# Two layers of a hybrid decoder trunk: scans moved out of the first inverse, and memory pieces dealt anew

## The reference

```python
for l in range(2):
  p = rmsnorm(x, norm_mix[l]) @ w_in[l]           # 1024 -> 3592 columns, split over four mixers
  y_a = hgrn2_mixer(...)      # group A: gated linear recurrence, 4 heads x 64
  y_b = gated_deltanet(...)   # group B: (I + lower) u = rhs per chunk of 64 tokens: a triangular inverse
  y_c = rglru_mixer(...)      # group C: h_t = a_t h_{t-1} + u_t, a = exp(-8 r softplus(-lambda))
  y_d = rwkv7_mixer(...)      # group D: decay w = exp(-exp(-0.5) sigmoid(.)), a second inverse
  x = x + concat(y_a, y_b, y_c, y_d) @ w_out[l]
  mem_n = rmsnorm(mem); k = mem_n @ wk[l]; v = mem_n @ wv[l]
  x = x + softmax(q k^T / 16) v @ wo[l]           # q = rmsnorm(x) @ wq[l], 4 heads x 256
  x = x + (swiglu(rmsnorm(x)) if l == 0 else top2_of_8_experts(rmsnorm(x)))
out = rmsnorm(x, norm_final)
```

## Time and profile before

| | us |
|---|---|
| median of 3 runs | 1963.12 (1962.64 to 1963.27) |
| profiled execution, own time | 1961.31 |
| its span, first to last instruction | 1959.5 |
| PE busy | 1861.4 (95%) |
| DVE busy | 1465.5 (75%) |
| ACT busy | 1121.3 (57%) |

### The profile page before, as it was taken

The page is one execution under the profiler, slowest core; times in us unless marked ns, Lnnn a source line. Parts: engine busy times, 40 slices in busy tenths (PEclk is TensorE's granted clock), DMA queues, the critical chain, the costliest instruction groups (busy, mean ns, idle before and its releaser), DMA issues.

```text
span 1959.5 us, 29713 instructions
## 1 busy us (share of the span) xinstructions
PE 1861.4 (95%) x12520; PEld 1605.6 (82%) x12521; DVE 1465.5 (75%) x1543; ACT 1121.3 (57%) x1057; POOL 0.2 (0%) x4
## 2 busy tenths in 40 slices
PE   7997899999999978999699999999999999999996
PEld 6986789899989866897588888888888888888884
DVE  6778645554467687453789989889899898998985
ACT  5563134434344641244567777677776777767774
POOL 0000000000000000000000000000000000000000
PEclk9998999999999989999899999999999999999998
DMA  7520234355555212243599999989999999999992
GB/s 243 172 75 15 66 108 165 108 181 185 194 157 164 89 45 66 74 164 111 184 393 342 373 330 384 370 335 371 337 383 365 335 372 348 369 364 339 369 373 97
DMA packets 239450, 465.99 MB, mean 238 GB/s; under 512 B 11856, under 2 KB 87760, under 8 KB 239312
## 3 DMA queue, kind: packets, MB, share of 16 engines
q1 hardware_dynamic: 239312, 464.03, 66.4%
HBM read 462.95 MB, written 1.05 MB: 237 GB/s over the span
## 4 chain that ended last, share of the span: by engine, by line
PE 88%; DVE 9%; issue 1%; ACT 1%; DMA 1%; DVEq 0%; SPq 0%; ACTq 0%
PE ps L2148 31%; PE ps L1617 16%; PE ps L2158 16%; PE ps L1602 12%; PE ps L1637 8%; DVE MT L907 2%; PE ps L2204 2%; PE ps L2179 1%; PE ps L1682 1%; PE ps L2219 1%; DVE MT L913 1%; DVE TMP L907 1%; DVE MT L910 1%; DMA raw<-in_w_in 1%; DVE spare_hi L907 0%
## 5 line engine op out<-in xcount | busy, mean ns | idle before, releaser
L1380 DVE TENSOR_TENSOR wlo<-raw,whi 128x2048 fp32r<-128x2048 f32 x140 | 320.5, 2292 | 55.7 <-ACT whi L787 55.4
L787 ACT ACTIVATE whi<-raw 128x2048 fp32r<-128x2048 f32 x140 | 268.9, 1922 | 121.1 <-PE ps L2158 71.3
L920 DVE TENSOR_TENSOR wlo<-raw,whi 128x2048 fp32r<-128x2048 f32 x85 | 194.6, 2289 | 85.3 <-ACT whi L480 85.1
L1380 DVE TENSOR_TENSOR wlo<-PT,whi 128x2048 fp32r<-128x2048 f32 x84 | 192.1, 2293 | 31.2 <-ACT whi L787 30.1
L480 ACT ACTIVATE whi<-raw 128x2048 fp32r<-128x2048 f32 x85 | 162.1, 1907 | 64.7 <-PE ps L1637 36.6
L2148 PE MATMUL ps<-whi,hE_hi 128*128 128x512 f32 x672 | 185.5, 398 | 2.4 <-DVE hE_lo L1449 2.4
L787 ACT ACTIVATE whi<-PT 128x2048 fp32r<-128x2048 f32 x84 | 161.5, 1922 | 34.9 <-PE ps L2148 34.2
L2148 PE MATMUL ps<-wlo,hE_hi 128*128 128x512 f32 x672 | 180.2, 390 | 0.0
L2148 PE MATMUL ps<-whi,hE_lo 128*128 128x512 f32 x672 | 179.9, 390 | 0.0
L2148 PEld LDWEIGHTS ps<-wlo,hE_hi 128*128 128x128 f32 x672 | 126.2, 188 | 27.1
L2148 PEld LDWEIGHTS ps<-whi,hE_lo 128*128 128x128 f32 x672 | 126.2, 188 | 26.5
(11 more groups left out here) (297 smaller groups left out, 3356.7 us busy)
## 6 DMA issues: line engine op xcount, KB each, us to landing
raw<-in_moe_w_up SPq DMA_DIRECT2D x111, 1024.0 KB, 7.0
PT<-in_moe_w_down SPq DMA_DIRECT2D x56, 1024.0 KB, 6.5
PT<-in_moe_w_gate SPq DMA_DIRECT2D x55, 1024.0 KB, 6.9
TMP<-in_moe_w_gate SPq DMA_DIRECT2D x55, 1024.0 KB, 6.8
raw<-in_moe_w_down SPq DMA_DIRECT2D x55, 1024.0 KB, 6.1
raw<-in_w_in SPq DMA_DIRECT2D x28, 1024.0 KB, 5.3
raw<-in_ffn_w_gate SPq DMA_DIRECT2D x11, 1024.0 KB, 5.3
raw<-in_ffn_w_up SPq DMA_DIRECT2D x11, 1024.0 KB, 5.7
```

The costliest lines, as they stand in the source:

```text
L787: nc.scalar.activation(ex_hi[m % XSPL], ex_raw[m % XRAW], ACT.Copy).then_inc(S("w_hi"), 1)
L920: V.tensor_tensor(wlo[i % SPL][:, :], raw[d % RAW][:, :], whi[i % SPL][:, :].bitcast(F32), ALU.subtract).then_inc(S("w_lo"), 1)
L1380: V.tensor_tensor(ex_lo[m % XSPL], ex_raw[m % XRAW], ex_hi[m % XSPL].bitcast(F32), ALU.subtract).then_inc(S("w_lo"), 1)
```

## The change

- **Group C's polynomial** (`rglru`) is renumbered: the slices that ran at v = 0 to 3 of the `hgrn` loop now run at j = 9, 10 and 11 behind the `w_in` chunks (as v = -4, -3, -2); one product moves from v = 4 to v = 6. The scan itself, with its output, moves from v = 4 of the first inverse to behind the second inverse, ahead of the split of `w_out` chunk 1, with a `chain.settle()` after it. Its buffers move from `whi` to `wlo` of the same slot.
- **Group D's decay scans** (one scaling, four scans, one small negation) move from v = 1 of the first inverse to j = 12, ahead of `logs`. The scaling K_KK moves from DVE to ACT.
- **Group A's outputs** go to PSUM bank 6 instead of 7, and ACT copies them to SBUF (`h_out`), so bank 7 is free for memory pieces.
- **Memory pieces.** Layer 1's piece order is v0, k0 to k3, v1 to v3. Its piece 0 is computed in the norm of layer 0's feed-forward part, its piece 1 in the first norm of layer 1: half before and half after the turning products. Piece 2 lies in the `hgrn` loop (half before it, one k step in v = 1 to 4), 3 and 4 in the first inverse, 5 in group B's solves, none in the second inverse, 6 and 7 as before. In layer 0 pieces 0 and 1 lie in the `hgrn` loop, 2 and 3 in the first inverse, 4 to 7 as before.
- **Start.** The table of small parameters is loaded by a transfer issued from ACT rather than SP, and the small activations of group C's lambda and group B's A_log, with two more table loads, run on ACT before the first statistics instead of in layer 0's `logs`; the six small DVE instructions behind them move to `rglru(l, -4)`.

The diff, cut to its core:

```diff
+PIECES = [[("xattn_wk", j) for j in range(4)] + [("xattn_wv", j) for j in range(4)],
+          [("xattn_wv", 0)] + [("xattn_wk", j) for j in range(4)] + [("xattn_wv", j) for j in range(1, 4)]]
 def plan_chunks():
...
+        if layer:
+            out += kv[1][1:2]
         out += [("cm", "w_in", layer, c) for c in W_IN_COLS]
-        out += pieces[0:4] + w_out[0:1] + pieces[4:6] + w_out[1:2] + pieces[6:7] + w_out[2:4] + pieces[7:8]
+        out += kv[layer][2 * layer:4 + layer] + w_out[0:1] + kv[layer][4 + layer:6] + w_out[1:2] + kv[layer][6:7] + w_out[2:4] + kv[layer][7:8]
...
         if layer == 0:
+            out += kv[1][0:1]
...
-        KV_BANK = [[7, 6, 7, 7, 7, 7, 2, 1], [7, 6, 7, 7, 7, 7, 2, 3]]
+        KV_BANK = [[7, 6, 7, 7, 7, 7, 2, 1], [3, 1, 7, 7, 7, 7, 2, 3]]
@@ ACT
-                a(tmp(5), ps[:, 7, :], ACT.Square).then_inc(S("o_sq"), 1)
-                act.wait_ge(S("rk_kk"), l + 1)
+                a(tmp(5), ps[:, 6, :], ACT.Square)
+                a(h_out(l), ps[:, 6, :], ACT.Copy).then_inc(S("o_sq"), 1)
+                for c in range(2):
+                    s_ = slice(256 * c, 256 * c + 256)
+                    a(K_KK[:, s_], pt(D_K)[:, s_], ACT.Copy, scale=pc("rwkv_k_k", l, c))
                 a(K_RN, K_KK, ACT.Square).then_inc(S("rk_sq"), 1)
...
             def deltanet(l):
+                kv_put(l, 2 + l)
                 rwkv_ahead(l)
...
+            act.dma_start(par[:, :], A["params"]).then_inc(S("par_in"), 16)
+            table("exp_and_others")
+            act.wait_ge(S("par_in"), 16)
+            for k in range(DEPTH):
+                o, o2 = PCOL["gdn_A_log", k][0], PCOL["lru_lambda", k][0]
+                a(col(lam[k], 2), par[:, o2:o2 + 2], ACT.Abs)
+                a(col(expa[k], 4), par[:, o:o + 4], ACT.Exp)
+                a(col(lam[k], 2), col(lam[k], 2), ACT.Exp, scale=-1.0)
+            table("natural_log")
+            for k in range(DEPTH):
+                a(col(lam[k], 2), col(lam[k], 2), ACT.Ln, bias=1.0).then_inc(S("lam_sp"), 1)
             table("sqrt_and_others")
@@ DVE, gates_ahead
+                    rglru(l, -4)
                 if j == 10:
+                    rglru(l, -3)
...
+                if j == 11:
+                    rglru(l, -2)
...
+                    dve.wait_ge(S("lora_s"), l + 1)
+                    ts(pt(C_X), pt(C_X), -float(np.exp(-0.5)), ALU.mult)
+                    for i in range(4):
+                        s_ = slice(P * i, P * i + P)
+                        chain.link(lambda: V.tensor_tensor_scan(K_B[:, s_], ones, pt(C_X)[:, s_], 0.0, ALU.mult, ALU.add))
+                    ts(col(ST_NC0, 4).unsqueeze(2), many(K_B)[:, :, HD - 1:HD], -1.0, ALU.mult)
                     logs(l)
@@ DVE, deltanet and rwkv
-                    if v == 4:
-                        rglru(l, LEVELS)
...
                 inverse(2 * l + 1)
+                rglru(l, LEVELS)
+                chain.settle()
                 ahead(first_chunk["w_out", l] + 2)
@@ PE, hgrn
-                kv(l, 0, range(KT // 2))
+                kv(l, 2 * l, range(KT // 2))
...
-                    if v < 5:
-                        kv(l, (v + 1) // 2, range(KT // 2) if v % 2 else range(KT // 2, KT))
+                    if l and 1 <= v < 5:
+                        kv(1, 2, [v + 3])
+                    if l == 0 and v < 2:
+                        kv(0, 0, range(5, 8) if v else [4])
+                    if l == 0 and 2 <= v < 6:
+                        kv(0, 1, [2 * v - 4, 2 * v - 3])
...
+                kv(l, 2 + l, [0])
@@ PE, first inverse
                     if v == 0:
+                        kv(l, 2 + l, [1])
                         head_ss(l, 0, tmp(5))
+                        kv(l, 2 + l, [2, 3])
                     if v == 1:
...
+                        kv(l, 2 + l, [4, 5])
+                    if v == 2:
+                        kv(l, 2 + l, [6, 7])
                     if v >= 3:
-                        pe.wait_ge(S("y_put"), 4 * l + 1)
-                        kv(l, 3, range(2 * v - 6, 2 * v - 4))
+                        pe.wait_ge(S("kv_put"), 2 * NH * l + 3 + l)
+                        kv(l, 3 + l, range(2 * v - 6, 2 * v - 4))
@@ PE, second inverse
-                    kv(l, 5, [v, v + 1] if v == LEVELS - 1 else [v])
+                    if l == 0:
+                        kv(0, 5, [v, v + 1] if v == LEVELS - 1 else [v])
@@ PE, norms
             def swiglu():
+                kv(1, 0, range(PRE))
                 pe.wait_ge(S("x_done"), 4)
                 norm(3)
+                kv(1, 0, range(PRE, KT))
...
+                if l:
+                    kv(1, 1, range(PRE))
                 norm(norm_index(l))
+                if l:
+                    kv(1, 1, range(PRE, KT))
```

More of the change, by code:

```diff
@@ L266, in lru, with h_out @@
         def lru(l, k):
-            return spare[0][(first_chunk["w_in", l] + 12) % SPL][:, 512 * k:512 * k + 512]
+            return spare[1][(first_chunk["w_in", l] + 12) % SPL][:, 512 * k:512 * k + 512]
+        def h_out(l):
+            return spare[0][(first_chunk["w_in", l] + 12) % SPL][:, 0:512]
         def h_state(l):
@@ L533, in gates_ahead @@
                     mem_norm(j)
+                if l and j == 1:
+                    kv_put(1, 1)
                 if j == 6:
@@ L592, in logs @@
                 a(col(ST_SP, 8), col(ST_SP, 8), ACT.Exp, scale=-1.0)
-                if l == 0:
-                    for k in range(DEPTH):
-                        o, o2 = PCOL["gdn_A_log", k][0], PCOL["lru_lambda", k][0]
-                        a(col(lam[k], 2), par[:, o2:o2 + 2], ACT.Abs)
-                        a(col(expa[k], 4), par[:, o:o + 4], ACT.Exp)
-                        a(col(lam[k], 2), col(lam[k], 2), ACT.Exp, scale=-1.0)
                 table("natural_log")
@@ L601, in logs @@
                     a(tmp(5), tmp(5), ACT.Ln, bias=1.0).then_inc(S("hg_ln"), 1)
-                    for k in range(DEPTH):
-                        a(col(lam[k], 2), col(lam[k], 2), ACT.Ln, bias=1.0)
                 else:
@@ L636, in hgrn @@
                         a(tmp(2), ps[:, 4, :], ACT.Exp).then_inc(S("gd_eg"), 1)
-                        kv_put(l, 0)
                     if v == 2:
@@ L647, in hgrn @@
                         rel_part(l, 0)
-                        kv_put(l, 1)
+                        if l == 0:
+                            kv_put(0, 0)
                     if v == 4:
@@ L654, in hgrn @@
                         a(h_kdt(l), ps[:, 5, 0:256], ACT.Copy).then_inc(S("hg_kd"), 1)
-                        kv_put(l, 2)
+                    if v == 6:
+                        kv_put(l, 1 + l)
                 table("natural_log")
@@ L700, in deltanet @@
                 ahead(first_chunk["w_out", l] + 1)
-                kv_put(l, 3)
+                kv_put(l, 3 + l)
                 for t in range(TT):
@@ L705, in deltanet @@
                 head_rms(l)
-                kv_put(l, 4)
+                kv_put(l, 4 + l)
                 ahead(first_chunk["w_out", l] + 2)
@@ L711, in rwkv @@
                 a(tmp(5), ps[:, 6, :], ACT.Copy).then_inc(S("rk_vk"), 1)
-                kv_put(l, 5)
+                if l == 0:
+                    kv_put(0, 5)
                 for t in range(TT):
@@ L762, in swiglu @@
                     ahead(n + SPL)
+                    if j == 0:
+                        kv_put(1, 0)
                     act.wait_ge(S("chunk_done"), n + 1)
@@ L1188, in hgrn, with head_out @@
                 take(LEVELS - 1)
-            def head_out(l, which, bank, o, gain, gate, pair):
+            def head_out(l, which, src, o, gain, gate, pair):
                 dve.wait_ge(S("o_rn"), 2 * l + which + 1)
-                tt(o, ps[:, bank, :], o, ALU.mult)
+                tt(o, src, o, ALU.mult)
                 for c in range(2):
@@ L1238, in rwkv_ahead @@
                         s_ = slice(256 * c, 256 * c + 256)
-                        ts(K_KK[:, s_], pt(D_K)[:, s_], pc("rwkv_k_k", l, c), ALU.mult).then_inc(S("rk_kk"), 1 if c else 0)
-                    for c in range(2):
-                        s_ = slice(256 * c, 256 * c + 256)
                         ts(K_KA[:, s_], pt(D_W)[:, s_], -1.0, ALU.add, pc("rwkv_k_a", l, c), ALU.mult)
                 if v == 1:
+                    dve.wait_ge(S("rk_sq"), l + 1)
                     stt(pt(D_K), K_KA, 1.0, pt(D_K), ALU.add, ALU.mult)
-                    ts(pt(C_X), pt(C_X), -float(np.exp(-0.5)), ALU.mult)
-                    for i in range(4):
-                        s_ = slice(P * i, P * i + P)
-                        chain.link(lambda: V.tensor_tensor_scan(K_B[:, s_], ones, pt(C_X)[:, s_], 0.0, ALU.mult, ALU.add))
-                    ts(col(ST_NC0, 4).unsqueeze(2), many(K_B)[:, :, HD - 1:HD], -1.0, ALU.mult)
                     tt(K_BM, K_B, pt(C_X), ALU.subtract).then_inc(S("rk_b"), 1)
@@ L1718, in gates_ahead @@
             def gates_ahead(l, j):
+                if l and j == 3:
+                    pe.wait_ge(S("kv_put"), 2 * NH + 2)
```

79 lines of the change are left out of this document (41 added, 38 removed).

## The result

The changed kernel took **1949.74 us** (median of four, 1944.4 to 1951.4) against 1963.03 for the kernel before beside it: ratio 0.9932, 95% interval 0.9918 to 0.9945. Five more rounds on another occasion gave 1945.37 (1944.7 to 1946.0) against 1961.28: 0.9918, 0.9905 to 0.9932. Predicted were 1946 and the range 1938 to 1955; as a change, 17.1 us less were forecast, and 13.3 and 15.9 were measured. The profiled execution took 1944.4, to 1944.2 predicted for it. One execution of a later experiment (the group C scan put back, 2110.84 us at a mean clock of 0.84) fell in a slower state of the chip and is in no median and no ratio.

The account below looks back on a forecast made before the run. PE was taken to bound the kernel (busy 95%; chain 88% PE, 9% DVE), with gains where DVE holds the chain. Terms -8.4 - 7.8 - 5.2 + 2.2 + 2.1 = -17.1 against 1963.1 gave 1946 us, range 1938 to 1955.

Parts of the forecast that it names:

- hgrn loop, -8.4: Loop of both layers: DVE loses scalings, one `ts` and four `stt`, staying the longer side; -4.2 us a layer.
- First inverse, -7.8: Both layers: DVE loses 7.3 us, PE gains eight k steps of 8.0 that cannot all hide; -3.9 a layer.
- both layers: Pricing of the first inverse: layer 0 and layer 1 alike, -3.9 us each.
- Second inverse, -5.2: Layer 1: k steps vanish, four masks gain 1.0 us each, v = 6 gains 0.1, about 1.2 behind the last level.
- -2 if PE runs the products at its lower clock: Layer 1's second inverse: the bound of smallest gain, -2 us, with products at PE's lower clock without fill.
- Norms, +2.2: Feed-forward norm and layer 1's first norm each take a memory piece: cost 1.5 + 0.7 us.
- Start, +2.1: Start: ACT begins the statistics at 10.2, 3.2 us late; 1.10 is slack, the rest reaches the chain.
- Group C scan behind the second inverse, 0: Moved scan of 4.16 us lies where DVE waited 5.36 for PE: cost 0 in layer 0, about 0.1 in layer 1.
- Rival 4: Mixers: TensorE loses its clock as fill leaves; fifteen slow levels cost 37 us, giving 1983; chance 0.06.
- A window of the mixers under 0.85: Sign in the changed trace: mixer windows showing a clock under 0.85 would mean the prediction is wrong.

Follow-up runs that it names:

- the useless products: Changed kernel with layer 1's memory piece 1 back in its hgrn loop, plus useless products in three levels of layer 1's second inverse: 1941.60 us.
- both pieces back: Changed kernel with all of layer 1's memory pieces dealt as in layer 0, both norms empty: 1944.68 us.

## Why the prediction was right, and where it wasn't

- **hgrn loop, -8.4:** measured -8.77. DVE is busy 27.2 us in the loop before and 23.3 after, close to the 4.0 that were counted, and PE's fill had room, even with eight useless steps more.
- **First inverse, -7.8:** measured -4.6, of which layer 0 -4.38 (predicted -3.9). Level by level layer 0 came out as forecast: up to the mask of v = 2 it gained 1.4 (predicted 1.2), v = 2 and 3 gained 0.9 (0.9), v = 4 gained 2.1 (2.0; mask to mask became 5.24, 175.29 to 180.53, predicted 5.3), v = 5 and 6 nothing (-0.2). Part of this is the clock, which rose from 0.89 to 1.00 over the stretch. **The step that failed is "both layers": layer 1 priced as layer 0.** Their loops do not hand over the same clock: layer 1's has 4 k steps and layer 0's 12, and that costs up to 3.2 us. With layer 0's dealing and the clock at 1.00 layer 1 gains 4.6 (43.0 us), in the traces at 0.96 it gains 3.1.
- **Second inverse, -5.2:** 4.1 of it lay before the last copy, where -3.15 was measured, and 1.2 behind, where +0.47 was: -2.7 in all. The bound "-2 if PE runs the products at its lower clock" described the mechanism: the clock is 0.52 from 761.2 to 771.8, one mask to mask is 5.14, and 0.51 from 788.8 to 792.3, just behind the last copy, where the 1.2 should have shown. With the useless products the first part is -4.6, the second still +0.5; about 1.0 of the 4.6 is clock that the kernel before had lost there (35.46, against 34.48 with steps put back). Later masks stand 3.4 apart as predicted (778.75 to 782.14), 3.9 where the transposes are.
- **Norms, +2.2:** measured +1.94 against the kernel before, all three windows at clock 1.00. It is 3.2 against the kernel with both pieces back, so part of the cost was hidden by the luck of the clock in the trace of before (0.78 in layer 1's norm). No load came late: PE has no wait from 358 to 400 and from 555 to 600.
- **Start, +2.1:** measured +0.27, and undoing it changes nothing. The parameters were there at 4.2 instead of 5.9, so the statistics began at 8.67 instead of the 10.2 that were forecast. The first turning product is 1.7 us later than before (11.32, 9.61), and by layer 0's loop all but 0.27 of that was absorbed, so the statistics were not what PE waited for longest:

```profile
4.23 0.44 ACT L480 ACTIVATE st<-par 128x2 f32<-128x2 f32 x2 [1.77 <-DMA par<-in_params]
...
5.63 1.28 ACT L477 ACT_TABLE_LOAD   x1
6.92 0.44 ACT L480 ACTIVATE st<-st 128x2 f32<-128x2 f32 x2
7.38 1.28 ACT L477 ACT_TABLE_LOAD   x1
8.67 1.06 ACT L480 ACTIVATE MT<-x 128x1024 f32<-128x1024 f32 x1
```

- **Group C scan behind the second inverse, 0:** right. DVE still waited for PE behind the split, 1.19 us in layer 0 and 1.70 in layer 1, so the 0.47 lost in layer 1 came from PE.

Summed, the terms missed by +3.2 (first inverse), +2.5 (second), -1.8 (start), -0.4 (loops) and -0.3 (norms), and two stretches where nothing had changed gave 1.3 (layer 0's second inverse) and 1.8 (experts). These cancel to within 0.2 us: the total is right by its terms for the loops, layer 0's inverse and the norms, and by luck for the rest. Rival 4, TensorE losing its clock in the mixers, was put at 0.06 as a loss of 37 us. Its mechanism was at work at about a sixth of that size: 4.4 us in layer 1's first inverse and about 1.4 in its second. A window of the mixers under 0.85 was named as a sign that the prediction is wrong, and it came: 0.82 over layer 1's loop and 0.84 over its second inverse (0.89 over its first). In the hgrn loop the slow PE was hidden, as the prediction said; it was paid one stage later.

The Trainium skill ("TensorE: Matmul & The Clock Gate", HAM oscillation) says that recurring idle gaps make the bursts behind them start at half clock. The trace agrees: 16 products in 2.08 us instead of 1.16 behind a loop in which PE was busy 19.2 of 27.7 us. Other traces differ: behind the same loop code the clock was 0.97 in one of them. The Trainium skill ("ScalarE: Activation LUTs", What ACT_TABLE_LOAD costs) adds a drain of about 1.38 us to each switch of table; in the five rows above each load takes 1.28 and the next activation begins 0.01 us behind it. The measurement decides: no such cost here.

What stays open: why three of the first four executions of the changed kernel and four of five with useless steps in the second inverse took 5 to 6 us more than their profiled ones. Their mean clocks are lower by 0.002 to 0.005, and 0.004 of 1945 us is 7.8 us of full-clock time, so the clock could explain it. It isn't the whole account: two executions with the scan put back took 1947.06 and 1951.44 us at the same mean clock of 0.982. Where the time was lost, no trace shows, and the transfers as a cause were not tested.

## What to carry to other kernels

Work that fills a matrix engine's waits is not only work that is hidden: it can also decide the clock of the stage behind it. When taking fill out of a loop that another engine bounds, price the next stage at both clocks, and check whether twin stages still leave the engine equally busy before pricing them alike. Where several executions of unchanged code differ by as much as the terms in question, compare stretches between the same two instructions over several traces, not totals.

## What the runs showed of the hardware

- The granted clock differs between executions of the same program. Layer 1's first inverse took 44.56, 47.42 and 47.81 us in three traces in which nothing ahead of it or in it differed, at 0.95, 0.89 and 0.88 of the full clock; layer 0's second inverse 34.1 or 35.6.
- Behind the same pause of 2.95 us on PE, 32 small products took 3.81 us in two traces and 5.27 to 6.76 in twelve.
- Eight k steps of useless fp32 products (8 us of PE) in a loop bounded by DVE cost that loop nothing measurable: 27.71 us with them, 27.72 without. In seven traces with a loop so filled the clock behind it was 1.00, in six without fill 0.54 to 0.97.
